# Block products of a split-precision ffn: high and low x beside each other in one 512-column matmul, low side weights by an adding DMA

## The reference, cut to what matters

```python
def swiglu(h, w_gate, w_up, w_down):
    return (jax.nn.silu(h @ w_gate) * (h @ w_up)) @ w_down
# first block, each of 2 layers: D_MODEL = 1024, D_FF = 2816, SEQ = 512
x = x + 0.5 * swiglu(rms_norm(x, ffn1_norm[l]), ffn1_wg[l], ffn1_wu[l], ffn1_wd[l])
...
x = x + 0.5 * swiglu(rms_norm(x, ffn2_norm[l]), ffn2_wg[l], ffn2_wu[l], ffn2_wd[l])
# second block: D_FF_2 = 4096
h = h + jnp.square(jax.nn.relu(u @ w_mlp1[l])) @ w_mlp2[l]
```

## Time and profile before

| | |
|---|---|
| time, median of 3 runs | 2506.87 us (2506.82 to 2506.97) |
| span of the profiled execution | 2505.1 us |
| TensorE busy, granted clock | 2490.8 us (99%), full in every slice |
| VectorE, ScalarE, GpSimd busy | 1961.7, 1232.5, 305.3 us |
| low side weights on VectorE, `whole_lo` in the ffns (L2323) | x140 |
| block products, L884 to L886 and L1447 to L1449 | 3 x (1960 + 336) matmuls of 256 columns |
| DMA | 246.87 MB, mean 99 GB/s |

### The profile page before, as it was taken

The page is one execution under the profiler, slowest core; times in us unless marked ns, Lnnn a source line. Parts: engine busy times, 40 slices in busy tenths (PEclk is TensorE's granted clock), DMA queues, the critical chain, the costliest instruction groups (busy, mean ns, idle before and its releaser), DMA issues.

```text
span 2505.1 us, 37038 instructions
## 1 busy us (share of the span) xinstructions
PE 2490.8 (99%) x14548; PEld 2204.3 (88%) x14548; DVE 1961.7 (78%) x2794; ACT 1232.5 (49%) x1963; POOL 305.3 (12%) x250
## 2 busy tenths in 40 slices
PE   9999999999999999999999999999999999999998
PEld 7999988889999889999888899998888888899997
DVE  7878867778888688887777888876899786877663
ACT  6444445444444454444553544445577535644442
POOL 4000001320000000000023100000187221200002
PEclk9999999999999999999999999999999999999999
DMA  5333332223333423333323233334333333233331
GB/s 157 98 96 100 100 105 84 82 85 102 96 108 102 118 79 104 96 106 114 102 64 95 74 103 105 104 104 135 91 72 82 126 92 111 83 108 99 99 100 59
DMA packets 487299, 246.87 MB, mean 99 GB/s; under 512 B 42321, under 2 KB 483926, under 8 KB 486870
## 3 DMA queue, kind: packets, MB, share of 16 engines
q1 hardware_dynamic: 486674, 244.19, 33.9%
q10 hardware_dynamic: 452, 0.32, 0.1%
HBM read 240.27 MB, written 4.19 MB: 98 GB/s over the span
## 4 chain that ended last, share of the span: by engine, by line
PE 96%; DVE 2%; ACT 1%; DMA 0%; issue 0%; POOL 0%; DVEq 0%; ACTq 0%
PE bank L886 8%; PE bank L885 8%; PE bank L884 8%; PE bank L767 6%; PE bank L768 6%; PE bank L769 6%; PE psS L906 4%; PE psS L907 4%; PE psS L908 4%; PE psT L950 2%; PE psT L952 2%; PE psT L951 2%; PE psT L767 2%; PE psT L769 2%; PE psT L768 2%; PE bank L1449 1%
## 5 line engine op out<-in xcount | busy, mean ns | idle before, releaser
L2254 DVE TENSOR_TENSOR wlo<-raw,whi 128x1024 fp32r<-128x1024 f32 (+2 forms) x212 | 288.7, 1364 | 49.9 <-ACT whi L1575 46.7
L767 PE MATMUL bank<-xhi,whi 128*128 128x512 f32 x672 | 264.5, 394 | 0.0
L768 PE MATMUL bank<-xlo,whi 128*128 128x512 f32 x672 | 261.9, 390 | 0.0
L769 PE MATMUL bank<-xhi,wlo 128*128 128x512 f32 x672 | 261.8, 390 | 0.0
L884 PE MATMUL bank<-xsh,whi 128*128 128x256 f32 x840 | 237.8, 283 | 0.0
L885 PE MATMUL bank<-xsl,whi 128*128 128x256 f32 x840 | 237.7, 283 | 0.0
L886 PE MATMUL bank<-xsh,wlo 128*128 128x256 f32 x840 | 237.7, 283 | 0.0
L1575 ACT ACTIVATE whi<-raw 128x1024 fp32r<-128x1024 f32 (+2 forms) x209 | 214.5, 1030 | 39.1 <-PE bank L769 22.1
L2317 DVE TENSOR_TENSOR wlo<-tw,whi 128x1024 fp32r<-128x1024 f32 x140 | 171.6, 1226 | 63.4 <-ACT whi L1615 63.3
L906 PE MATMUL psS<-hhi,whi 128*128 128x512 f32 x488 | 191.7, 393 | 0.0
L907 PE MATMUL psS<-hlo,whi 128*128 128x512 f32 x488 | 191.6, 393 | 0.0
(11 more groups left out here) (709 smaller groups left out, 7280.5 us busy)
## 6 DMA issues: line engine op xcount, KB each, us to landing
raw<-in_ffn_wg SPq DMA_DIRECT2D x88, 512.0 KB
raw<-in_ffn_wu SPq DMA_DIRECT2D x88, 512.0 KB
raw<-in_w_in SPq DMA_DIRECT2D x53, 512.0 KB
raw<-in_w_mlp SPq DMA_DIRECT2D x40, 512.0 KB
raw<-in_ffn_wd SPq DMA_DIRECT2D x48, 256.0 KB
raw<-in_ffn_wd SPq DMA_DIRECT2D x24, 448.0 KB
raw<-in_ffn_wd SPq DMA_DIRECT2D x48, 192.0 KB
raw<-in_ffn_wd SPq DMA_DIRECT2D x48, 128.0 KB
```

The costliest lines, as they stand in the source:

```text
L767: pe.matmul(dest, a, rhs_hi(k), start=start and k == 0, stop=False)
L768: pe.matmul(dest, a, rhs_lo(k), start=False, stop=False)
L769: mm = pe.matmul(dest, b_, rhs_hi(k), start=False, stop=stop and k == tiles - 1)
L2254: dve.tensor_tensor(wlo[:, a:a + n], raw[:, a:a + n], whi[:, a:a + n].bitcast(F32), ALU.subtract).then_inc(s_split, 1)
```

## The change

High x and low x are put side by side in SBUF, so that one matmul of 512 columns can read 256 columns of each (`paired`). A k step is then two matmuls: high weights by both, into both halves of a bank, and low weights by high x, 256 columns, into the first half. All banks and partial copies are 512 columns wide, and VectorE adds the two halves of each result (a fold). bank[0]'s second half goes through one more copy on ScalarE (`k_sn` 4g + 4), since VectorE adds it to the first half in PSUM. The low parts of the side rows are no longer subtracted by VectorE: ScalarE writes the negated high part to `wlo`, and a DMA issued by GpSimd adds `raw` to it. `part[2]` lies in other memory, and the semaphores of the memory norm are shared with those of v.

```diff
-        xhi = sb("xhi", KC * S, F32R)
-        xlo = sb("xlo", KC * S, F32R)
+        xhl = sb("xhl", 2 * KC * S, F32R)
+        xhi, xlo = xhl[:, 0:KC * S], xhl[:, KC * S:2 * KC * S]
...
+        paired = lambda a, lo: a[:, :].rearrange("p (h n) -> p h n", h=2)[:, :, lo:lo + QT]
+        folds = lambda a: a.rearrange("p (h n) -> p h n", h=2)
...
+                    if w:
+                        sp.wait_ge(k_sl[i], 16 * (net.first_g + w))
...
-                        mh, ml = moving(k)
-                        pe.matmul(dest, a, mh, start=start and k == 0, stop=False, skip_group_check=resumed)
-                        pe.matmul(dest, a, ml, start=False, stop=False, skip_group_check=resumed)
-                        mm = pe.matmul(dest, b_, mh, start=False, stop=stop and k == 3, skip_group_check=resumed)
+                        mhl, mh = moving(k)
+                        pe.matmul(folds(dest), a, mhl, start=start and k == 0, stop=False, skip_group_check=True)
+                        mm = pe.matmul(dest[:, 0:QT], b_, mh, start=False, stop=stop and k == 3, skip_group_check=True)
...
-                    pe.wait_ge(k_lo, 4 * g + 3)
+                    pe.wait_ge(k_sl[0], 16 * (g + 1))
                     side(w, 0).then_inc(s_used, 1)
...
                     act.activation(whi[:, a:a + n], raw[:, b_:b_ + n], ACT.Copy).then_inc(s_hi, 1)
+                    act.activation(wlo[:, a:a + n], raw[:, b_:b_ + n], ACT.Copy, scale=-1.0).then_inc(k_nh, 1)
...
-                    act.activation(part[1][:, :], bank[0][:, 0:QT], ACT.Copy).then_inc(k_sn, 1)
+                    act.activation(part[1][:, :], bank[0][:, :], ACT.Copy).then_inc(k_sn, 1)
                     if on:
                         sums_hi(w + 1, 0)
                         whole_hi(w + 1, 0)
...
+                    act.wait_ge(s_used, q0 + c0 + u + 3)
+                    act.wait_ge(k_ev, 7 * g + 4)
+                    act.activation(part[1][:, 0:QT], bank[0][:, QT:S], ACT.Copy).then_inc(k_sn, 1)
                     if on:
                         sums_hi(w + 1, 1)
...
-                    dve.tensor_tensor(tmp[1][:, t1], psT[:, 0:QT], part[0][:, :], ALU.add).then_inc(k_ev, 1)
-                    whole_lo(w, 1)
+                    dve.tensor_tensor(part[0][:, :], psT[:, 0:S], part[0][:, :], ALU.add).then_inc(k_ev, 1)
+                    dve.wait_ge(k_ev, 7 * g + 1)
+                    dve.tensor_tensor(tmp[1][:, t1], part[0][:, t1], part[0][:, t2], ALU.add).then_inc(k_ev, 1)
...
-                    dve.tensor_tensor(tmp[3][:, t2], bank[1][:, 0:QT], part[1][:, :], ALU.add).then_inc(k_ev, 1)
+                    dve.wait_ge(k_ev, 7 * g + 3)
+                    dve.tensor_tensor(tmp[3][:, t2], part[1][:, t1], part[1][:, t2], ALU.add).then_inc(k_ev, 1)
                     side_adds(w, 0)
-                    if on:
-                        whole_lo(w + 1, 0)
...
-                    dve.tensor_tensor(tmp[1][:, t2], bank[0][:, 0:QT], inv[:, t2], ALU.mult).then_inc(k_ev, 1)
-                    dve.wait_ge(k_ev, 4 * g + 1)
-                    dve.tensor_tensor(tmp[1][:, t1], tmp[1][:, t1], inv[:, t1], ALU.mult).then_inc(s_gs, 1)
+                    dve.wait_ge(k_sn, 4 * g + 4)
+                    dve.tensor_tensor(tmp[1][:, t2], bank[0][:, 0:QT], part[1][:, t1], ALU.add).then_inc(k_ev, 1)
+                    dve.wait_ge(k_ev, 7 * g + 5)
+                    dve.tensor_tensor(tmp[1][:, :], tmp[1][:, :], inv[:, :], ALU.mult).then_inc(s_gs, 1)
...
-                    dve.tensor_tensor(tmp[3][:, t1], bank[1][:, 0:QT], part[2][:, :], ALU.add).then_inc(k_ev, 1)
-                    dve.wait_ge(k_ev, 4 * g + 4)
+                    dve.tensor_tensor(part[2][:, :], bank[1][:, :], part[2][:, :], ALU.add).then_inc(k_ev, 1)
+                    dve.wait_ge(k_ev, 7 * g + 6)
+                    dve.tensor_tensor(tmp[3][:, t1], part[2][:, t1], part[2][:, t2], ALU.add).then_inc(k_ev, 1)
...
+            def sides_lo(first, cols):
+                for w in range(len(cols)):
+                    for i in range(2):
+                        a, b_, n = (2 * i + 1) * UNIT, (2 + i) * UNIT, cols[w][i]
+                        pool.wait_ge(k_nh, 2 * (first + w) + i + 1)
+                        pool.dma_start(wlo[:, a:a + n], raw[:, b_:b_ + n], accum_op=ALU.add).then_inc(k_sl[i], 16)
```

More of the change, by code:

```diff
@@ L194, in build @@
         dwl = sb("dwl", S, F32R)
-        part = [sb(f"part{i}", QT) for i in range(3)]
+        part = [sb(f"part{i}", S) for i in range(2)]
         assert at[0] <= nc.sbuf_usable_end, (at[0], nc.sbuf_usable_end)
         top = at[0]
+        paired = lambda a, lo: a[:, :].rearrange("p (h n) -> p h n", h=2)[:, :, lo:lo + QT]
+        folds = lambda a: a.rearrange("p (h n) -> p h n", h=2)
+        part.append(sb("part2", S, off=first_inv.manual_sbuf_range[0]))
+        assert cvec.manual_sbuf_range[0] >= identr.manual_sbuf_range[0] + 4 * S
+        mlp_part = part[:2] + [sb("mlp_part2", S, off=identr.manual_sbuf_range[0])]
         at[0] = region
@@ L450, in build @@
         k_lo = sem("fast_weights_lo_ready")
+        k_nh = sem("side_weights_hi_negated")
+        k_sl = [sem(f"side_weights_lo_landed{i}") for i in range(2)]
         k_pe = sem("fast_product_done")
@@ L746, in _ @@
             for m in range(KC):
-                load(C_MLP + MLAST_AT + m, 0, c2(t["w_mlp2_2"], *MGROUPS[-1], m * P))
+                c = C_MLP + MLAST_AT + m
+                slot_free(c, 0)
+                if slot(c) in SIDE_SLOTS and m < RING:
+                    sp.wait_ge(k_sl[SIDE_SLOTS.index(slot(c))], 16 * (FIRST_G + MFAST))
+                sp.dma_start(dst(c, 0, mlp_tiles(-1)), c2(t["w_mlp2_2"], *MGROUPS[-1], m * P)
+                             ).then_inc(landed[slot(c)], LANDED)
             ov = out.rearrange("o (i p) d -> p (o i) d", p=P)
@@ L1687, in fast_window @@
                     if g:
-                        act.wait_ge(k_ev, 4 * g - 3)
-                    act.activation(part[0][:, :], bank[0][:, 0:QT], ACT.Copy).then_inc(k_sn, 1)
+                        act.wait_ge(k_ev, 7 * g - 5)
+                    act.activation(part[0][:, :], bank[0][:, :], ACT.Copy).then_inc(k_sn, 1)
                     if w == 0:
@@ L2206, in mlp_window @@
                     mlp_whole_hi(w + 1, 0)
+                else:
+                    for j in range(AHEAD - 1):
+                        mlp_ahead(MLAST_AT + j)
+                act.wait_ge(s_used, C_MLP + WINDOWS_AT + 4 * w + 3)
+                act.wait_ge(k_ev, 7 * g + 4)
+                act.activation(part[1][:, 0:QT], bank[0][:, QT:S], ACT.Copy).then_inc(k_sn, 1)
+                if on:
                     mlp_sums_hi(w + 1, 1)
                 else:
-                    for j in range(AHEAD):
-                        mlp_ahead(MLAST_AT + j)
+                    mlp_ahead(MLAST_AT + AHEAD - 1)
                 mlp_square(f, tmp[1], tmp[1])
@@ L2249, in _, with split @@
         def _(dve):
-            def split(c, q, tiles=8):
+            def split(c, q, tiles=8, units=1):
                 dve.wait_ge(s_hi, q + c + 1)
@@ L2338, in ahead @@
                     else:
-                        split(c0 + u, q0, UNIT_TILES.get(u, 8))
+                        split(c0 + u, q0, UNIT_TILES.get(u, 8), 2 if u == LAST_AT else 1)
                 def quarter_sums(i):
@@ L3086, in mlp_ahead @@
                 elif u < MLAST_AT + KC:
-                    split(C_MLP + u, 0)
+                    split(C_MLP + u, 0, 8, 2 if u == MLAST_AT else 1)
             def mlp_quarter_sums(i):
@@ L3372, in _ @@
                 pool.tensor_tensor(acc[:, :], acc[:, :], tmp[2 + m % 2][:, :], ALU.add).then_inc(s_sq, 1)
+            sides_lo(FIRST_G, [[len(MSIDES[w, i]) * P for i in range(2)] for w in range(MFAST)])
             squares(FINAL1 + 3, FINAL1 + 3, KC - 1, more=1)
```

225 lines of the change are left out of this document (114 added, 111 removed).

## The result

After: 2590.27 us median (2589.73 to 2591.33, 4 runs); before, in the same runs, 2506.92 us (2506.82 to 2506.98, 4 runs). The ratio is 1.0333, with a 95% interval of 1.0321 to 1.0345: 83 us slower. The prediction was 2574 with a range of 2538 to 2610.

The account below looks back on a forecast made before the run. TensorE was taken to bound the kernel before, a loop over VectorE and ScalarE after. Ffns two to four +63, first ffn -1, +2 and +7, MLP -4: +67 on the profiled 2505.1, 2574 as runs' median; range 2538 to 2610.

Parts of the forecast that it names:

- The bound moves from TensorE to the loop that ends in the part[0] copy: Ffn windows: the first sum product waits for ScalarE's part[0] copy, 1.26 us late, 1.43 with the restart.
- The walk: Step-by-step loop from T, the third sum product's end: part[0] copy done at T + 11.44, T back after 15.93 us.
- The wait ahead of the dwh product: With 3 tiles in the first side, TensorE waits about 0.3 us for the add that empties bank[1].
- The k step: TensorE's matmuls per step: 0.347 us after against 0.360, 0.013 less in 2296 steps, 30 us if nothing else moved.
- MLP -4: Last MLP's 12 windows hide the same loop, no stall or up to 0.2 us: 4 us less.
- Ffn one +8: First ffn: five TensorE-bound or tied windows -1, five with 8 tiles +2, six with 6 or 7 tiles +7 us.
- Ffns two to four +63: 54 windows, 14.63 us before and 15.8 after: 63 us more.
- The adding DMA hidden: GpSimd's DMA for the side rows takes between 1 and 7 us, under some 10 us of cover: 0 us.
- TensorE stays the bound: Rival: the loop is at least 1.4 us a window shorter than walked, only the matmul saving counts: 2477 us, chance 0.06.

Follow-up runs that it names:

- e1: Changed kernel, but in the ffn windows ScalarE makes the second side piece's negated twin behind the part[0] copy, not ahead of it: 2562.01 us.
- e2: Changed kernel, but ScalarE's fourth copy sn4 writes tmp[0], so it no longer waits for VectorE's fold: 2581.18 us.
- e4: Changed kernel with part[0] copy first on ScalarE, sn4 in tmp[0], VectorE's add and fold of bank[1] ahead of the first sums' low part: 2508.79 us.
- e12: e11 with VectorE's second sums' low part behind the hidden product instead of ahead of it, in the ffns: 2486.57 us.
- e11: e8 with the next window's last weight block taken ahead of the silu and the second sums' low part, in the ffns: 2525.6 us.
- e8: e4 with each block product's four merged 512-column matmuls first and its four 256-column ones behind, instead of in turn: 2505.98 us.
- e9: e4 with merged matmuls reading 512 columns in one run and writing a bank as one run, low x left out: 2508.38 us.
- e10: e8 with the first fold of each ffn window on GpSimd instead of VectorE: 2509.2 us.

## Why the prediction was right, point by point

- *The bound moves from TensorE to the loop that ends in the part[0] copy*: shown. Taking single members out gives back what they cost (e1 28 us, e2 9 us), and another order of the same work, with sn4's own buffer, gives 81 us (e4). Added up from the starts in after's trace: 80 us ahead of the first sum products, 5 for the late second matmul behind them, 14 ahead of the dwh products, less 15 for the merged matmuls, is 84, for 84.4 between the two spans.
- *The walk*: copies, sums and adds stood within 0.04 us of their steps up to T + 3.6. Then one step was too short: sn4 started at T + 4.19, not 3.99, since with 4 tiles in the first side TensorE's last corner product ends later than the fold; the hidden copy followed at T + 9.51, not 9.24. That the copy still ended at T + 11.44, as walked, is luck: the walk priced side and twin at 4 tiles (11.22 with 3), and the two differences cancel. From T to T over the windows of after but each ffn's first, ordered by the tiles of a window's first side and of the copied second side of the next:

| first side, copied side | windows | mean us from T to T | walked |
|---|---|---|---|
| 3, 3 | 24 | 15.92 | 15.7 |
| 3, 4 | 9 | 16.12 | 15.93 |
| 4, 3 | 10 | 16.04 | 15.7 |
| 4, 4 (the window that was walked) | 15 | 16.25 | 15.93 |

  So the loop was right in its members and 0.2 to 0.3 us too short in each form. Where the first side has 3 tiles, sn4 follows the fold as walked (T + 4.06), and what is left is 0.1 us by the part[0] copy's end and 0.1 behind it, where three products in turns stand.
- *The wait ahead of the dwh product*: right. With 3 tiles in the first side it starts 0.36 to 0.42 us behind the matmul ahead of it, where its turn is 0.12; the prediction had about 0.3. TensorE's table of waits hardly shows it (1.5 us, 3 times).
- *The k step*: mis-sized. 0.347 was taken from rows in which each width follows its own kind. In turns the pair takes 0.353, and grouped 0.349. The gain of TensorE's own work is 6.7 ns a step and not 13, 15 us in all and not 30; the side tiles' matmuls give a little of it back (231.7 ns on the mean in e4 for 229.3), so that a TensorE-bound window of e4 is 0.13 us shorter than before, and of e12 0.27. The Trainium skill ("TensorE: Matmul & The Clock Gate", section "Wait — 56ns, not 53.3ns?") has 2.5 ns for the edit, and the measured 6.7 lies between that and mine.
- *MLP -4*: the same term, and nine of its windows start the first sum product 0.08 to 0.16 us late, 0.9 us in all; it gave 0.4.
- *Ffn one +8*: it took 13 more. The first five windows, forecast to be TensorE's own (-1), took 2.6 more. In the second to the fifth, with 5 tiles in the first side, sn4 waits for the last corner until T + 4.9, which makes the loop 17.0 to 17.2 and not 16.2: the same step as above. The first took 0.95 of the 2.6, and not by this loop: TensorE waits 0.9 us there for the part[2] copy (L1712), which stands behind two 5-tile copies, the hidden copy and the corner's; e4 and e12 have that wait too (1.0 us).
- *Ffns two to four +63*: 72.5. The mean of 15.8 was too low, it is 16.0, by the 0.2 to 0.3 us of the table above. By window starts the lengths look uneven (many windows that took 14.20 take 15.2 to 15.3, and many that took 14.88 take 16.3 to 16.6); that comes of where the window is cut, since the wait ahead of its sum product belongs to the loop that began in the window before. With ffn one (5 over its forecast) and the MLP (3.6), this makes the 17.5 us between the span of after, 2589.5, and the 2572 that the prediction had for it.
- *The adding DMA hidden*: right. Issue and landing in after (KB each, median us from issue to landing):

```profile
wlo<-raw POOLq DMA_DIRECT2D x80, 192.0 KB, 3.5
wlo<-raw POOLq DMA_DIRECT2D x52, 256.0 KB, 4.1
```

  Inside the bounds of 1 and 7 us, with some 10 us of cover; no wait of TensorE in a window is put down to a DMA. The Trainium skill ("DMA: Bandwidth & Descriptors", section "Anatomy of one DMA — SWDGE (gpsimd) path") gives 2.5 us, an estimate from its figures; the trace has 1.0 to 1.5 more.
- *The rival "TensorE stays the bound", 2477*: false for the change, and nearly true of what the same products make possible (2486.6, e12). Of the 10 us between, the k step of 349.1 for 347 makes 5 (2296 x 0.0021) and the side tiles' 1464 matmuls in the ffns, 230.2 ns on the mean for 229.3 before, 1. The wait in the first window of ffn one makes another 1.2 (17.23 us, where its own work would be 16.03). The other 3 are not accounted for.

## What to carry to other kernels

An edit that takes work from the bounding engine and adds some to two others is decided by the queue order on those two: walk the loop that returns to the bound, in each form that it takes (one form's walk can agree with another form's time by chance), and before giving the edit up, put each copy that the bound waits for at the head of its group. After each opened loop, look again for the next one; here there were three, and one move without its partner (e11) made it worse by 20 us. A matmul's price is to be read where its neighbours have the width that they will have.

## What the runs showed of the hardware that I had not expected

- In e4 a 512-column matmul behind a 256-column one starts its successor after 232 to 241 ns. In e8, grouped, the four take 227 behind a side product and 224 to 236 (232.4 on the mean) in the five products behind 256-column ones; the 256-column ones take 113 to 121. The operand's two runs, 4096 columns apart, cost nothing that shows (e9).
- A 256-column add on GpSimd that starts no later than 0.08 us behind a 1024-column VectorE subtraction takes 0.94 to 1.09 us and makes the subtraction 2.0 to 2.3 instead of 1.22; started 0.17 us behind it or later, the add takes 1.56 to 1.65 and the subtraction its 1.22 (e10, 66 windows).
- An adding DMA in SBUF costs GpSimd 0.86 us to issue and lands 192 KB in 3.5 and 256 KB in 4.1 us (medians in after; 4.3 and 4.2 in e4, 3.1 and 3.4 in e12).
- After a stall, the second matmul too is late, as in the earlier trace rows: 1703.72 - 1703.41 = 0.31 from the merged matmul's start to the next, where 0.235 is its turn, so a short wait costs TensorE 0.07 to 0.1 us on top.
